# Latent-head attention: the second half of a head's query rotation, its sum, its roundings and its remainders one slot further up

## The reference, cut to what matters

```python
def mla_attention(c_q, c_kv, k_rope, positions, q_norm_g, kv_norm_g, w_uq, w_ukv):
    q = (rmsnorm_2(c_q, q_norm_g) @ w_uq).reshape(B, S, MLA_HEADS, MLA_QK_DIM)
    q = jnp.concatenate([q[..., :MLA_NOPE_DIM], rope(q[..., MLA_NOPE_DIM:], positions)], axis=-1)
    q = q * (MLA_QK_DIM ** -0.5)
    kv = (rmsnorm_2(c_kv, kv_norm_g) @ w_ukv).reshape(B, S, MLA_HEADS, MLA_NOPE_DIM + MLA_V_DIM)
    ...
    s = jnp.einsum('bqhd,bkhd->bhqk', q_blk, k).astype(jnp.float32)
    p = jax.nn.softmax(s, axis=-1).astype(v.dtype)
    return jnp.einsum('bhqk,bkhd->bqhd', p, v)
```

## Time and profile before

| | |
|---|---|
| median of three runs | 2958.82 us |
| the three runs | 2952.75, 2958.82, 2961.45 us |
| the profiled execution, its own time | 2957.47 us |
| its span (first to last instruction) | 2955.6 us |
| PE busy | 2838.3 us, 96% of the span |
| DVE busy | 1857.6 us, 63% |
| ACT busy | 1178.2 us, 40% |
| mean granted TensorE clock | 0.983 |

### The profile page before, as it was taken

How to read it: one execution, slowest core, us unless ns; L and a number is a source line. 1 busy time by engine, 2 the same in 40 slices (tenths; PEclk the granted TensorE clock), 3 DMA queues, 4 the chain that set the end, 5 groups by cost and what they waited for, 6 DMA issues and landing times.

```text
span 2955.6 us, 36741 instructions
## 1 busy us (share of the span) xinstructions
PE 2838.3 (96%) x13910; PEld 2278.8 (77%) x13910; DVE 1857.6 (63%) x2418; ACT 1178.2 (40%) x1948; POOL 720.5 (24%) x493
## 2 busy tenths in 40 slices
PE   7989999899999999997999999999999999999998
PEld 6778777678877888886789766668788888877887
DVE  2583566675597656655877488840656665686568
ACT  2232555434034333322344366631454454444313
POOL 2414111211542000000003500014334343450254
PEclk8999999999999999998999999999999999999999
DMA  3102000133443222227233300013332223223453
GB/s 132 40 22 84 19 22 22 46 116 114 162 157 122 89 83 86 86 74 295 94 114 96 97 15 15 15 45 112 86 85 77 77 76 82 68 75 114 154 181 114
DMA packets 118238, 263.27 MB, mean 89 GB/s; under 512 B 13504, under 2 KB 26560, under 8 KB 113984
## 3 DMA queue, kind: packets, MB, share of 16 engines
q1 hardware_dynamic: 70432, 143.44, 15.0%
q10 hardware_dynamic: 47648, 117.62, 11.8%
HBM read 196.01 MB, written 52.43 MB: 84 GB/s over the span
## 4 chain that ended last, share of the span: by engine, by line
PE 76%; DVE 14%; ACT 4%; issue 2%; DMA 1%; POOL 1%; ACTq 1%; POOLq 0%; SPq 0%; DVEq 0%
PE ps L394 13%; PE ps L2739 13%; PE ps L339 8%; PE ps L1934 7%; PE ps L1964 6%; PE ps L3102 5%; PE ps L1134 3%; PE ps L2324 2%; PE ps L3311 2%; PE ps L1151 1%; PE ps L1176 1%; PE ps L1153 1%; PE ps L378 1%; PE ps L1152 1%; PE ps L3568 1%
## 5 line engine op out<-in xcount | busy, mean ns | idle before, releaser
L4355 POOL TENSOR_TENSOR wh<-raw,zeros 128x512 fp32r<-128x512 f32 x232 | 285.3, 1230 | 1549.6 <-PE ps L394 561.0
L4357 POOL TENSOR_TENSOR wl<-raw,wh 128x512 fp32r<-128x512 f32 x232 | 402.7, 1736 | 18.2
L394 PE MATMUL ps<-hth,wh 128*128 128x512 f32 x704 | 286.5, 407 | 2.1 <-DVE fox_vl L1358 2.1
L394 PE MATMUL ps<-hth,wl 128*128 128x512 f32 x704 | 280.1, 398 | 0.0
L394 PE MATMUL ps<-htl,wh 128*128 128x512 f32 x704 | 279.7, 397 | 0.0
L3175 POOL TENSOR_TENSOR lat_wh<-raw,zeros 128x416 fp32r<-128x416 f32 x8 | 7.6, 955 | 648.3 <-DVE htl L2962 643.4
L394 PEld LDWEIGHTS ps<-hth,wh 128*128 128x128 f32 x704 | 133.5, 190 | 32.0 <-issue 3.0
L394 PEld LDWEIGHTS ps<-htl,wh 128*128 128x128 f32 x704 | 133.2, 189 | 32.5
L394 PEld LDWEIGHTS ps<-hth,wl 128*128 128x128 f32 x704 | 133.9, 190 | 26.1
L339 PE MATMUL ps<-wh,hth 128*128 128x512 f32 (+1 forms) x320 | 123.8, 387 | 4.1 <-DVEq L305 1.5
L2739 PE MATMUL ps<-htl,up_wh 128*128 128x512 f32 x320 | 126.1, 394 | 0.0
(11 more groups left out here) (623 smaller groups left out, 7961.8 us busy)
## 6 DMA issues: line engine op xcount, KB each, us to landing
raw<-in_stream_dram SPq DMA_DIRECT2D x240, 256.0 KB, 2.6
up_raw<-in_stream_dram SPq DMA_DIRECT2D x21, 1024.0 KB, 5.7
htl_f<-in_stream_dram SPq DMA_DIRECT2D x31, 512.0 KB, 3.7
merge_raw<-in_stream_dram SPq DMA_DIRECT2D x12, 1024.0 KB, 7.0
merge_sg_dram<-merge_sg ACTq DMA_DIRECT2D x12, 1024.0 KB, 5.8
merge_sg<-merge_sg_dram ACTq DMA_DIRECT2D x12, 1024.0 KB, 4.8
dil_stg<-dil_stg ACTq DMA_DIRECT2D x96, 128.0 KB, 2.4
ff_dram<-ff SPq DMA_DIRECT2D x20, 512.0 KB, 3.0
```

The source lines that it names most:

```text
L394: ins = nc.tensor.matmul(ps[:, bank + half, :], w[:, j, c:c + P], a[:, k, HALF * half:HALF * half + HALF], start=k == 0 and q == 0, stop=k ...
L4355: nc.gpsimd.tensor_tensor(wh[:, s, :], raw[:, s, :], zeros[:].to_broadcast([P, HALF]), ALU.add).then_inc(w_hi, 1)
L4357: nc.gpsimd.tensor_tensor(wl[:, s, :], raw[:, s, :], wh[:, s, :], ALU.subtract).then_inc(w_split, 1)
```

## The change

In the loop's preparation of a head, five DVE instructions and two ACT instructions go one slot earlier: `ta1`, `tb1` and `qn1` from offset -13 to -14, `x1` and `ql1` from -12 to -13, `qm1` and `qp1` from -11 to -12. In places: from 3, 4, 5 to 2, 3, 4. PE's list is unchanged. No instruction is added or removed, and no wait.

```diff
-                    return (flat(at(-17, "qn0", "qp0"), at(-13, "qn1"), at(-11, "qp1"), at(-10, "kh0"), at(-8, "kh1")),
+                    return (flat(at(-17, "qn0", "qp0"), at(-14, "qn1"), at(-12, "qp1"), at(-10, "kh0"), at(-8, "kh1")),
                             flat(at(-19, "ta0", "tb0"), at(-18, "x0"), at(-17, "ql0"), at(-16, "qm0"),
-                                 at(-13, "ta1", "tb1"), at(-12, "x1", "ql1"), at(-11, "qm1"), at(-10, "kl0"), at(-8, "kl1")),
+                                 at(-14, "ta1", "tb1"), at(-13, "x1", "ql1"), at(-12, "qm1"), at(-10, "kl0"), at(-8, "kl1")),
...
-                for h in self.at(-13, s):
+                for h in self.at(-14, s):
                     self.queries_high(act, h, 1)
-                for h in self.at(-11, s):
+                for h in self.at(-12, s):
                     self.rotated_high(act, h, 1)
...
+                for h in self.at(-14, s):
+                    self.rotation(dve, h, 1)
                 for h in self.at(-13, s):
-                    self.rotation(dve, h, 1)
-                for h in self.at(-12, s):
                     self.rotation_sum(dve, h, 1)
                     self.queries_low(dve, h, 1)
-                for h in self.at(-11, s):
+                for h in self.at(-12, s):
                     self.rotated_low(dve, h, 1)
```

## The result

The changed kernel takes **2967.9 us** (median of 7, 2964.01 to 2973.99) against 2955.12 us for the kernel before (median of 7, 2952.44 to 2961.45): ratio **1.0041**, 95% interval 1.0029 to 1.0052, that is 12.1 us slower (8.6 to 15.4). Its profiled execution has a span of 2966.7 us, 11.1 more than before. The base of the forecast was the median of the first three runs, 2958.82 us; the median of seven lies 3.7 lower.

The account below looks back on a forecast made before the run. PE sets the pace on average, with DVE's list binding places 2 to 6. Losses of 0.99, 3 x 1.31 and 3 x 1.18 sum to 8.5 us over the base median, giving 2967.3 us, range 2960 to 2977.

Parts of the forecast that it names:

- Step 1: PE's wait at `k0` for `ql1`, 0.52 us a head, can go; with the values' wait at most 5.3 us gained.
- What bounds the kernel: DVE's list bounds places 2 to 6 of each prepared head; everywhere else in the head PE is ahead.
- Step 2: On DVE, `ta1` and `tb1` delay the maximum of place 3 to 3.91 us after the maximum of place 2 starts.
- Step 3: At the end of place 4, PE's row transpose waits some 1.5 us for the delayed maximum of place 3.
- Step 4: ACT's row copy queues behind `qp1`, which waits for `x1`; PE stalls 0.87 us before the scores of place 6.
- The sign that I had named for it: PE's L1134 would show a wait of about 0.7 to 0.9 us for ACT L1073, seven times.
- Step 5: M, from the place 2 maximum's start (the mark) to PE's place 7 scores: 9.88 us in even heads, before 8.57.
- Nothing gives it back: The 8.5 us lost over seven heads stay lost: by place 9 maxima wait for PE again, later stages follow PE.
- Rival (a): PE's clock also falls in one to five heads, 1.7 us each: 2969 to 2976 us; chance 0.24.
- (b): The row copy is not late, as ACT reaches it ahead of `x1`: 4.6 us lost, 2963.4 us; chance 0.13.
- (c): The products fit beside DVE's waits for PE at places 2 and 3: up to 5.3 us faster, 2953.5; chance 0.06.
- (d): It cancels: PE waits elsewhere for the same end of DVE's list, within 2 us, 2957 to 2961; chance 0.05.

Follow-up runs that it names:

- e4: Kernel before, with the output multiply of units ending at place 15 moved from place 2 to 5 on DVE, the ACT send behind it; 2954.57 us, one execution.
- e1: Changed kernel, with ACT's row copy put ahead of the preparation of its slot, so no longer queued behind `qp1`; 2963.87 us, one execution.
- e2: Kernel before, with only `qp1` moved one slot earlier on ACT, to place 4 ahead of the row copy; 2985.56 us, one execution.
- e7: Kernel before, with key projection `k0`, its rounding and its remainder one slot later, at place 7; 2960.49 us, one execution.
- e5: Kernel before, with both rotation products of a half as one DVE multiply and an added ACT copy; 2949.70 us against 2956.72, ratio 0.998.
- e3: Kernel before, with only `x1` and `ql1` moved one slot earlier on DVE, right behind `tb1`; 2954.29 us, one execution.

## Why the prediction was right, point by point

The forecast was 2967.3 us, 8.5 us slower, by a new wait of PE. The median is 2967.9, the stage lost 9.6, and every step is in the trace. That the two times agree to 0.6 us is luck, though: the forecast stood on a base of 2958.82, and against the base of seven runs, 2955.12, the loss is 12.8 by the medians and 12.1 by the ratio. What is well met is the mechanism and the 9.6 of the stage.

- *Step 1* (the wait at `k0` goes): right; no wait for L3505 is left.
- *What bounds the kernel:* that PE is ahead everywhere else in a head was not so. Of the sixteen waits at the values only seven were in the stretch, and seven more, of some 0.20 each, come once a head right behind the other row (1720.58, 1721.17 in the kernel before). Nothing in the sum hung on it, since nine are left after the change.
- *Step 2* (the two products push the maximum of place 3 by their full length): right in its numbers, 3.91 forecast and 3.91 measured. Its reading of the kernel before was too simple: the stretch was not DVE's list from the maximum of place 2, but PE's raw scores up to 2.3 after the mark and DVE's list only from the maximum of place 3 (e4). The result was the same since the multiply had filled the gap exactly. Where I said that the price of the multiply was 0.13 in even heads by the rule of the Trainium skill on start quadrants (VectorE: DVE Perf Modes, "Two Vector instructions with no wait between them"), the trace agrees: behind `tb1` it starts 0.73 later, and the maximum 0.60 behind it (1808.05, 1808.78, 1809.38).
- *Step 3* (PE waits 1.5 us at the row): right, 1.51 in head 4, 1.18 in head 1 and 1.5 to 1.7 in the others, 10.7 us in all.
- *Step 4* (the row copy is queued behind `qp1` and comes late): right. ACT's wait 2.37 against 2.3 in even heads; in odd ones it is 1.05, since the late exponentials stand ahead of it and are done before `x1`, as foreseen. The second stall is 0.82 to 0.83 (0.91 in head 1) against the 0.87 of the forecast, which by its own terms, 6.85 to 7.75, was 0.90. e1 takes the cause away and gets the 0.77 back; e2 makes the cause alone and the scores start at 8.46 where 8.4 was worked out. The sign that I had named for it, PE waiting for ACT L1073, is not in the profile of the changed kernel, which names the remainder ending 0.04 to 0.05 us later; by that sign I would have called a right step wrong.
- *Step 5*, the term that was mis-sized: the start of the scores behind the row copy, 0.15 us after its end and not 0.03 (0.10 in head 1). M came out at 10.02 for head 4 where 9.88 was worked out, and over the seven heads the loss is 9.6 rather than 8.5; this term is 0.8 of the 1.1. In head 1 a second one of 0.11 joins it: with no multiply between, the remainder starts 1.25 behind the maximum of place 3 (1701.10, 1702.35) and not 1.14. The 0.03 was a distance from DVE to ACT; my rows held none from ACT to PE.
- *Nothing gives it back:* right; M's sum over seven heads (9.6) is the stage's loss (9.6).
- *Rival (a)*, the clock: not in the traced execution of the changed kernel, whose stalls of 1.2 to 1.7 and 0.8 to 0.9 kept it at 1.00 in all seven heads. It is close, though: e1, with a stall of 1.2 to 1.7 and a short one, lost it in one head of seven, e2 with 3.00 in every stretch, and the same two waits at the start of the stage cost seven traces of ten their clock and the other three nothing. So the forecast's choice of "none" is borne out by one execution only; the stretch at 1687 that it leaned on was one of the three. Whether (a) has a part in the other six executions, no trace shows.
- *Rivals (b), (c), (d)*: (b) is what e1 shows, at 9.25: apart from head 5's clock, e1 loses 4.2 us to the kernel before, where (b) had 4.6. (c) and (d) did not happen, and in e7, with no DVE work pushed forward, the 0.5 a head was spent again one slot later.

The other 2 to 3 us between the stage's 9.6 and the ratio's 12.1 are not explained; they lie within the ratio's interval (8.6 to 15.4) and within the scatter of the rest of the span.

## What to carry to other kernels

Before moving an instruction up an in-order queue, list what it now stands in front of on each engine and what those wait for: here the moved steps were early enough for their own consumer already, and the cost came from a maximum and a one-row copy that had stood ahead of them. An instruction that must itself wait belongs behind a short copy that is ready and that another engine needs (e1 gets 4 to 5 of the 9.6 us back by that alone). And an instruction with no idle ahead of it is not shown to be bound by its own queue, since its input may have come just then. Where one engine's list is the stretch, taking an instruction out of it (e5) gives its full length, while the reorderings tried here (e3, e7 and the change itself) only changed who waits.

## What the runs showed of the hardware

- A stall of 3.00 us before a burst of matmuls left PE at 1.2 GHz afterwards (0.43 us a matmul instead of 0.23) in all seven heads of e2; stalls of 1.51 and 0.82 in the changed kernel did not in seven heads of one trace, and 1.66 in e1 did in head 5 and not in head 3. Waits of 1.3 and 0.7 at the start of the stage, the same in all ten traces, did in seven and not in three: the length of a stall alone does not decide. In e2 the stalls and the clock behind them cost about twice what was worked out for the stalls.
- The clock came back while PE worked without a pause: in head 4 of e2 matmuls are 0.43 apart from 1818.82 to 1824.37 and 0.23 from 1824.71 on. The Trainium skill says that activity releases the throttled state (TensorE: Matmul & The Clock Gate, "Part 1"); the trace agrees.
- From the end of an ACT copy to the start of PE's waiting matmul 0.14 to 0.15 us went by in heads 2 to 7 of the changed kernel and of e2 (0.10 in head 1), where from DVE to PE it was 0.05 to 0.06 at `k0` and at the row (1809.00 to 1809.05 in the kernel before). Behind the row copy of head 0 in the kernel before it was 0.04 (1687.58 to 1687.62); why the one is short and the other long is open.
- The releaser in the profile is the producer that ended last before the wait's end, not always the one waited for: with two ends 0.04 to 0.05 us apart it named the wrong one seven times.
- A DVE multiply costs the same over 64 partitions as over 32 (0.71 and 0.70 us for 512 columns).
